# The order of the records of a split weight tile in TensorE's projections, and the place of the wait for GpSimd

## The reference, cut to what matters

```python
proj = h @ p['w_in']                       # q, k, v, GLA parts, glu, gates
y_att = o_att @ p['w_att_o']; y_gla = o_gla @ p['w_gla_o']; y_conv = ... @ p['w_conv_o']
return (g_att * y_att + g_gla * y_gla + g_conv * y_conv) @ p['w_out']
(silu(h @ p['w_ff_gate']) * (h @ p['w_ff_up'])) @ p['w_ff_down']
# block two: h @ w_in_2, mix @ w_out_2, h @ w_up_2, ... @ w_down_2
```

## Time and profile before

| | |
|---|---|
| median of 3 runs | 2996.16 us (2993.62 to 2996.81) |
| the profiled execution, its own time | 3002.65 us |
| its span in the trace | 3000.9 us |
| PE busy | 94% of the span, 19004 matmuls |
| POOL busy | 46% |
| ACT, DVE busy | 44% each |
| TensorE clock granted, mean | 0.976 of full |

### The profile page before, as it was taken

One profiled execution on the slowest core, in us unless ns is written; L12 is line 12 of the kernel. 1 busy time (PEld: TensorE's weight loads), 2 busy tenths in 40 slices (PEclk: granted clock), 3 DMA queues, 4 the chain that ended last, 5 costly groups with the idle time before them and its releaser, 6 DMA issues.

```text
span 3000.9 us, 45357 instructions
## 1 busy us (share of the span) xinstructions
PE 2813.7 (94%) x19004; PEld 2414.5 (80%) x19004; DVE 1306.7 (44%) x2717; ACT 1310.4 (44%) x2204; POOL 1382.3 (46%) x646
## 2 busy tenths in 40 slices
PE   7999998899999999998999999999998899988998
PEld 5778876688876788886878799989986799876898
DVE  3777857532333211104676753332137442174440
ACT  3254433323424422224464346454454465445563
POOL 3432030244431534443531267668762488632786
PEclk9999999999998999999999999999999999998999
DMA  6332022132324343334320245435543255432454
GB/s 237 121 106 81 29 78 82 46 119 92 119 84 157 121 139 128 119 99 166 124 71 22 64 133 156 148 129 182 182 120 120 78 183 175 137 121 84 137 180 123
DMA packets 103555, 359.48 MB, mean 120 GB/s; under 512 B 11127, under 2 KB 17527, under 8 KB 102841
## 3 DMA queue, kind: packets, MB, share of 16 engines
q1 hardware_dynamic: 103352, 356.60, 37.0%
HBM read 355.51 MB, written 1.05 MB: 119 GB/s over the span
## 4 chain that ended last, share of the span: by engine, by line
PE 79%; DVE 9%; ACT 6%; POOL 3%; DMA 1%; issue 1%; SPq 0%; ACTq 0%; DVEq 0%
PE PS L358 79%; POOL RINGL L2516 2%; ACT AR L1161 2%; DVE AR L1795 1%; ACT AR L1690 1%; ACT WH L1141 1%; DVE AR L1799 1%; DMA RING<-w_ada_in 1%; ACT L1161 1%; DVE AR L1956 1%; DVE SM L1795 1%; ACT XT L1161 1%; DVE SM L2029 1%; DVE AR L2400 1%; DVE ARR L1795 1%
## 5 line engine op out<-in xcount | busy, mean ns | idle before, releaser
L2516 POOL TENSOR_TENSOR RINGL<-RING,WH 128x1024 fp32r<-128x1024 f32 (+1 forms) x554 | 1300.7, 2361 | 1507.3 <-ACT WH L1141 1506.6
L358 PE MATMUL PS<-HTR,WH 128*128 128x256 f32 (+2 forms) x2736 | 876.0, 321 | 0.0
L1141 ACT ACTIVATE WH<-RING 128x1024 fp32r<-128x1024 f32 (+1 forms) x554 | 568.6, 1035 | 643.2 <-PE PS L358 518.5
L358 PE MATMUL PS<-HTH,WH 128*128 128x256 f32 (+1 forms) x2336 | 748.3, 322 | 25.8 <-POOL RINGL L2516 20.6
L358 PE MATMUL PS<-HTH,RINGL 128*128 128x256 f32 (+1 forms) x2336 | 727.2, 317 | 4.1 <-POOL RINGL L2516 4.1
L358 PE MATMUL PS<-ARR,WH 128*128 128x256 f32 (+2 forms) x2688 | 691.8, 325 | 16.5 <-ACT WH L1141 5.8
L358 PEld LDWEIGHTS PS<-HTR,WH 128*128 128x128 f32 (+1 forms) x2736 | 524.1, 192 | 40.2 <-issue 2.1
L358 PEld LDWEIGHTS PS<-ARR,WH 128*128 128x128 f32 (+1 forms) x2688 | 467.3, 191 | 63.2 <-issue 15.2
L358 PEld LDWEIGHTS PS<-HTH,WH 128*128 128x128 f32 x2336 | 449.4, 192 | 66.5 <-issue 20.5
L358 PEld LDWEIGHTS PS<-HTH,RINGL 128*128 128x128 f32 x2336 | 444.7, 192 | 33.6 <-POOL RINGL L2516 5.4
L358 PE MATMUL PS<-ARR,RINGL 128*128 128x256 f32 (+1 forms) x1472 | 466.3, 327 | 1.5 <-POOL RINGL L2516 1.5
(11 more groups left out here) (195 smaller groups left out, 3395.5 us busy)
## 6 DMA issues: line engine op xcount, KB each, us to landing
RING<-w_ada_in SPq DMA_DIRECT2D x96, 512.0 KB, 3.7
RING<-w_up_in SPq DMA_DIRECT2D x88, 512.0 KB, 4.2
RING<-w_gates_in SPq DMA_DIRECT2D x48, 512.0 KB, 3.6
RING<-w_ff_gate_in SPq DMA_DIRECT2D x44, 512.0 KB, 3.7
RING<-w_ff_up_in SPq DMA_DIRECT2D x44, 512.0 KB, 3.6
RING<-w_glu_in SPq DMA_DIRECT2D x32, 512.0 KB, 4.5
RING<-w_ff_down_in SPq DMA_DIRECT2D x32, 512.0 KB, 3.5
RING<-w_in_in SPq DMA_DIRECT2D x32, 512.0 KB, 3.6
```

The source lines that it names most:

```text
L358: return e.matmul(out_, lhsT, rhs, start=start, stop=stop)
L1141: e.activation(RINGS[name][:, j, 0:width], RING[:, b % NSLOT, 0:width], ACT.Copy).then_inc(*a_upper.up(b))
L2516: e.tensor_tensor(RINGL[:, i, 0:width], RING[:, i, 0:width], RINGS[name][:, j, 0:width], ALU.subtract).then_inc(*g_lower.up(b))
```

## The change

In `project`, `project_tok`, the gate projection, `mix_rows` and `mix_rest`, `load` now waits for the upper part only. The upper products of the whole block come first (sixteen in a full block), then a wait for `g_lower`, then its eight lower products, the last of which signals `p_block` as before. The number of matmuls, their operands and their banks are the same. `group` and the programs of the other four engines are the same.

```diff
@@ project
-                    n, up, low = load(A[name][l, ct, :, k0 * P:(k0 + k) * P], k * P)
+                    n, up, low = load(A[name][l, ct, :, k0 * P:(k0 + k) * P], k * P, lower=False)
                     for i, j in enumerate(order[0:k]):
                         kt = k0 + j
                         pe.wait_ge(*ready(kt))
                         w = slice(j * P, j * P + P)
                         mm(o, up[:, w], hi(kt, cols), k0 + i == 0, False)
                         mm(o, up[:, w], lo(kt, cols), False, False)
+                    pe.wait_ge(*g_lower.to(n))
+                    for i, j in enumerate(order[0:k]):
+                        kt = k0 + j
+                        w = slice(j * P, j * P + P)
                         last = mm(o, low[:, w], hi(kt, cols), False, k0 + i == kt_total - 1)
                     last.then_inc(*p_block.up(n))
@@ gla_projections, gate projection
-                n, up, low = load(A["w_glr"][l], 256)
+                n, up, low = load(A["w_glr"][l], 256, lower=False)
                 for kt in range(8):
                     pe.wait_ge(*ready(kt))
                     w = slice(kt * 32, kt * 32 + 32)
                     mm(o, up[:, w], hi(kt, BOTH), kt == 0, False)
                     mm(o, up[:, w], lo(kt, BOTH), False, False)
+                pe.wait_ge(*g_lower.to(n))
+                for kt in range(8):
+                    w = slice(kt * 32, kt * 32 + 32)
                     t = mm(o, low[:, w], hi(kt, BOTH), False, kt == 7)
...
```

More of the change, by code:

```diff
@@ L435, in project_tok @@
                 for q in range(8 // per):
-                    n, up, low = load(A[name][l, g * (8 // per) + q, :, 0:per * width], per * width)
+                    n, up, low = load(A[name][l, g * (8 // per) + q, :, 0:per * width], per * width, lower=False)
                     pe.wait_ge(*ready(per * q + per - 1))
@@ L443, in project_tok @@
                             mm(o, lo(kt, x), up[:, w], False, False)
+                    pe.wait_ge(*g_lower.to(n))
+                    for o, t in zip(os_, tiles):
+                        o, x = o[:, 0:width], slice(t * P, t * P + P)
+                        for j in range(per):
+                            kt, w = per * q + j, slice(j * width, (j + 1) * width)
                             last = mm(o, hi(kt, x), low[:, w], False, kt == 7)
@@ L922, in mix_rows @@
                         bank(3 + i, "w_mix", l, i, until=(a_mix, "fsq", l, "w_mix", i))
-                b, up, low = load(A["w_mix_k"][l, n], 1024)
+                b, up, low = load(A["w_mix_k"][l, n], 1024, lower=False)
                 pe.wait_ge(*d_mix.to("mp", l, kt))
@@ L928, in mix_rows @@
                     mm(o, up[:, w], MP2[1](kt, X), False, False)
+                pe.wait_ge(*g_lower.to(b))
+                for ct in range(8):
+                    o, w = banks[3 + ct // 2][:, 256 * (ct % 2):256 * (ct % 2) + 256], slice(ct * P, ct * P + P)
                     t = mm(o, low[:, w], MP2[0](kt, X), False, False)
@@ L938, in mix_rest @@
                     if i < 4:
-                        b, up, low = load(A["w_mix_c"][l, i], 1024)
+                        b, up, low = load(A["w_mix_c"][l, i], 1024, lower=False)
                         for j in range(8):
@@ L945, in mix_rest @@
                             mm(o, up[:, w], MP2[1](kt, X), False, False)
+                        pe.wait_ge(*g_lower.to(b))
+                        for j in range(8):
+                            kt, w = 2 + j % 4, slice(j * P, j * P + P)
+                            o = banks[3 + i][:, 256 * (j // 4):256 * (j // 4) + 256]
                             t = mm(o, low[:, w], MP2[0](kt, X), False, j == 7)
```

## The result

The changed kernel takes 2964.2 us in the median of 4 executions (2961.97 to 2965.38), beside 2995.5 us for the kernel before on the same chip: 31.3 us less, a ratio of 0.9886 with a 95% interval of 0.9872 to 0.9899. The forecast was 2973.0, in a range from 2964 to 2988. Direction and mechanism held; the gain is 8 us larger than the 23 us forecast.

The account below looks back on a forecast made before the run. PE was taken to bound the kernel, busy 94% of the span. Waits saved 21.9 + clock 3.3 - held back 2.0 = 23 us, so from the median 2996.2 - 23 = 2973 us, range 2964 to 2988.

Parts of the forecast that it names:

- the heads: Sixteen block starts outside groups where PE waits for POOL's lower part; starting on the upper part saves 21.9 us.
- The 512-column heads: Heads at 393.10 and 567.20: wait cut to that for ACT, 2 x 2.35 = 4.7 us, clock gain apart.
- the gate projection: Head at 1456.03: PE's late start behind POOL's 256-wide lower part goes whole, 2.9 us, clock gain apart.
- the pair at 1860: Heads at 1860.77 and 1869.57: count once, 1.92 us, since ACT brings the second's upper part late anyway.
- The zero for the seams: Some 530 blocks get a wait between upper and lower products; its cost was taken as nothing.
- Three of these waits are followed by matmuls at half clock: Behind 393.10, 567.20 and 1456.03: less half clock (1.2 GHz) after shorter pauses, together 3.3 us.
- Whole wait saved: Heads at 906.71, 2198.78 and its repeat, four of 1.12 us and one of 0.16: whole wait goes, 6.6 us.
- the rival: Slower: the wait at each seam stops PE's stream, 0.10 us each, 53 us in all, 3026 us; chance 0.05.
- 1930.78: A 256-column head: wait of 2.02 us cut by 1.92 us, when the block asks for its lower part.
- the rival held back: Gains ahead of stretches bound by a loop of engines are lost there: gain 11.8, time 2984.4; chance 0.18.
- Take 2 us off: Ahead of GLA and attention stretches, where PE also waits for ACT and DVE: 2 us of gain held back.
- The rival with more clock: Another tenth of the half-clock stretches all over the kernel goes, 7 us more, time 2966; chance 0.10.

Follow-up runs that it names:

- with fillers: The kernel before with small matmuls on constants filling seven of PE's long waits for POOL: 2995.9 us, ratio 0.9995 to the kernel before.
- heads only: The change made in the sixteen head blocks alone, the old form in all others: 2971.1 us, 0.991 of the kernel before.
- the kernel with five: The change in the sixteen heads and the five blocks behind each (88 blocks): 2966.3 us, 0.9902 of the kernel before.
- all but the heads: The change in all blocks outside the groups but the sixteen heads, which keep the old form: 2996.7 us, 1.0001 of the kernel before.
- the two repeats: The changed kernel run again twice, nothing altered: 2963.8 us and 2964.7 us, both 0.989 of the kernel before.
- Two followers: The change in the sixteen heads and the next two blocks behind each: 2970.7 us, 0.9916 of the kernel before; on another chip 2972.3, 0.9919.

## Why the prediction was right and wrong

**Right.** The sign, the place and the mechanism: order and wait together, at the heads, and nothing in long steady stretches. The 512-column heads (6.6 us predicted with their clock, 6.9 measured in two of three profiles), the gate projection (4.3 and 4.45) and the pair at 1860 (1.92 and 1.95) came as worked out. The zero for the seams held. PE's waits for POOL went to 6.3 us, where 6 to 9 were foretold; those for ACT rose by 6.9, not 3: the pair's waits for ACT (0.44 and 2.31 us) were in the sum but not in that sentence, and the pauses of 2.7 and 1.6 us that the prediction itself leaves at the first two heads are more than 3 already. POOL's pace of one block in 2.34 us was too fast for blocks in a row behind the norm of 1930.78 (2.52), but PE's 2.88 still leaves it ahead, as the sum needs.

**Wrong: the sum, by 8 us of 31.** Term by term, from the table:

- "Three of these waits are followed by matmuls at half clock": there were six. The one at 1860.77 costs nothing, as PE waits again at 1869.57 for POOL, and POOL for ACT, whatever PE did in between: half clock from 1861.8 to 1865.2 in the kernel before, none with fillers, and 0.00 us between the two. But the heads at 2212.23 and 2618.86 pay it as well, some 1.2 us after their start, where I had not looked. Windows of the kernel before, before and in that stretch (columns of rows 5):

```profile
2209.00:2212.20 3.20, 1.27 (x11) 1.07 (x9) 0.00 (x0) 3.17 (x5) 2.38 (x2) 1.00 0.61 177
2212.20:2213.40 1.20, 1.17 (x10) 1.17 (x11) 0.00 (x0) 0.00 (x0) 1.20 (x1) 0.99 0.80 321
2213.40:2216.80 3.40, 3.40 (x18) 3.18 (x17) 0.00 (x0) 0.00 (x0) 3.40 (x2) 0.50 0.02 6
```
```profile
2213.16 0.28 PE L358 MATMUL PS<-HTR,WH 128*128 128x256 f32 x1
...
2213.60 0.42 PE L358 MATMUL PS<-HTR,WH 128*128 128x256 f32 x1
2213.82 0.41 PE L358 MATMUL PS<-HTH,RINGL 128*128 128x256 f32 x1
```

  Starts are 0.21 us apart there, and 0.12 before. Sixteen such matmuls cost 16 x 0.09 = 1.4 us more. In the changed kernel the clock stays at its full level through the whole place:

```profile
2177.00:2180.00 3.00, 3.00 (x28) 3.00 (x27) 0.00 (x0) 2.96 (x5) 1.11 (x1) 1.00 0.62 183
2180.00:2183.40 3.40, 3.39 (x29) 3.19 (x27) 0.17 (x1) 3.36 (x5) 2.40 (x2) 1.00 0.62 167
```

  Measured 3.33 and 3.42 for 1.92 each: 2.9 us more. The Trainium skill ("TensorE: Matmul & The Clock Gate", section "Wait — 56ns, not 53.3ns?") has matmuls of N columns N ÷ 1.2 GHz apart at the lower clock, 427 ns for 512 columns; 213 ns for 256 is an estimate by that rule. The trace agrees, with 0.21 here and 0.43 behind 567.20.
- "Whole wait saved": a stop costs more than its idle time. At 2198.78 the row says 0.62 us idle, but the start before it is 2197.78 and the one behind it 2199.12, so two steps of 0.227 took 1.34 us: 0.89 lost. The idle time is counted from the modelled end of a matmul, after the next would have started (0.39 - 0.227 = 0.16 us), and the restart costs 0.10 us; I had that 0.10 in hand as a price of the rival, and left it out of the gain. Six heads of this kind (1.12, 0.62, 0.60) gained 7.35 us in the first profile against 5.7: 1.65 more.
- 1930.78: 1.92 predicted, 2.84 measured. 1.87 of it is there right behind the head, as worked out; 0.96 comes in the norm that follows, which the clock held down in the kernel before and holds down for less long now (0.74 in the second profile). Windows over the same work, before and after:

```profile
1957.40:1967.40 10.00, 9.31 (x126) 7.51 (x127) 3.25 (x6) 5.82 (x12) 0.00 (x0) 0.50 0.01 2
```
```profile
1932.90:1942.90 10.00, 9.23 (x129) 7.98 (x126) 3.17 (x6) 5.05 (x10) 0.00 (x0) 0.66 0.01 2
```

- 906.71: 0.71 predicted, -0.17. With heads only it is there, 1.28. In the changed kernel the clock behind the `w_out` group's wait at 879.13 is down for longer:

```profile
881.00:885.00 4.00, 4.00 (x11) 3.12 (x10) 0.00 (x0) 0.00 (x0) 0.42 (x1) 0.50 0.00 0
```

  The same place in the kernel before (887.78) is back at 1.00 from 893 on, 5.2 us behind its wait. That is 0.9 us less than forecast. PE's idle time fell by the 0.71 foretold, so it is not a loop of engines that took it, as in the rival held back, but the clock. In the kernel with five there is no half clock in this stretch, and it gains 2.65.
- The 567 and 1456 heads gave 0.3 and 0.15 more, the 0.16 of the smallest head nothing.
- "Take 2 us off": behind the heads nothing of it is seen; from 2300 to 2367 the changed kernel loses 1.0 us in two profiles (3.9 in the third), and three stretches without a head of their own (977, 2401 and 2816) give 1.2 back (all but the heads has 0.8 of that). So 2.2 us more than forecast.

23.2 forecast + 2.9 + 1.65 + 0.9 - 0.9 + 0.3 + 2.2 = 30.3 us, against 31.3 measured, 33.2 and 32.5 in the two repeats. The last 1 to 3 us I cannot place: they are less than what profiles of one kernel differ by. The balance is no proof to the last microsecond either: which of the stretches without a head to count in it (the 2.2) is my choice, and some 10 us of the first profile's gain are left out of it as belonging to the single execution of before.

**The step that failed most** was the clock's term: priced only at the three heads of the earlier trace rows, it stood at 3.3 us and came to some 6.6 (3.3 + 2.9 + 0.9 - 0.9 and 0.45 at 567 and 1456), or 8 by the mean clocks. A gain of 2 us of idle is worth 3.4 where half clock follows it. Second is the price of a stop, 1.65 us, third the 2 us taken off. What decides whether half clock follows a wait, no run here shows.

**What I had not said at all**: that a head's gain depends on the blocks behind it. My sum held because they were changed too; that was luck, as I had not asked. Two followers give no more time than none in the medians (2970.7 and 2972.3 against 2971.1), where the table has 2.4 and 3.7 us more; the intervals, 4 us either way, allow both. In the table they win at the waits behind heads (1400, 1852, 1975, 2193, 2387, 2590, 2776: 5.3 us over heads only), and lose 0.8 to 1.0 us at 1425 and 1.5 at 2150, in both profiles. The first is the third block behind the group, whose wait starts just ahead of the border of the table's rows, and short stops at the blocks after it; the two rows together give 0.25 with heads only, 0.55 with two and 1.35 in the changed kernel:

```profile
1408.12 0.36 PE L359 MATMUL PS<-ARR,WH 128*128 128x256 f32 x1 [0.39 <-POOL RINGL L2538]
```

The second is a wait for a POOL part of the norm that neither heads only nor the changed kernel has there. Why it comes is open:

```profile
2164.04 0.37 PE L359 MATMUL PS<-WH,HTH 128*128 128x284 f32 x1 [2.03 <-POOL HTR L2549]
```

The rival with more clock (2966) was nearest to the result, and by the right cause in part: its 7 us were to come from stretches all over the kernel, and came, as far as the table shows, mostly behind the heads.

## What to carry to other kernels

Price a wait by starts, from the last matmul before it to the second behind it, and look at the granted clock for several microseconds behind every such wait, not only where the matmuls next to it are slow; then take the clock's part as the less certain one, since half clock can come up behind another wait. Where an operand comes in two parts and one is late, put all work on the early part first and the wait behind it; and give the same order to the next five blocks or so, since the producer is still behind and each follower in the old order asks for its part at once. A satisfied wait in the middle of such a matmul stream may be taken as free.

## What I had not expected of the hardware

- 952 satisfied waits on PE cost nothing that shows: 2961.5 us with them, 2964.7 without.
- The granted clock can fall some way behind a wait and not in it. At 393.10, a wait of 5.1 us, it fell inside; at 2212.23, one of 1.95 us, it is full during the wait and for 1.2 us behind it, and 0.50 only from 2213.40 on, when PE is busy again.
- Plain float32 fillers appear as two records each in the profile, 0.11 us apart with 128 columns, so keeping the clock up by them is easy to overdo: the clock rose from 0.976 to 0.984 and the time stayed at 0.9995 of before.
- Filling some waits moved the half clock as well as removing it: two waits of 1.11 us that had full clock behind them have 0.50 in the filled kernel, at 1.4 us each.
